# Expert stage: weights in 8 KB rows, six half-unit slots, the whole down projection in split fp32r, the next expert's tokens transposed and split one expert ahead

## The reference

```python
def expert_choice_ffn(h, w_router, w_gate, w_up, w_down):
    B, N, D = h.shape                                    # 1, 1024, 1024
    cap = EC_CAPACITY_FACTOR * N // N_EXPERTS            # 128
    aff = softmax(einsum('bnd,de->bne', h, w_router), axis=-1)
    gates, idx = lax.top_k(aff.swapaxes(1, 2), cap)
    xe = h[bidx, idx]
    hid = silu(einsum('becd,edf->becf', xe, w_gate)) * einsum('becd,edf->becf', xe, w_up)
    ye = einsum('becf,efd->becd', hid, w_down) * gates[..., None]
    return zeros_like(h).at[bidx, idx].add(ye)
...
        x = x + g2 * expert_choice_ffn(...)
    return rms_norm(x, final_norm_g)
```

## Time and profile before

| | us |
|---|---|
| median of three runs | 2294.64 |
| the runs | 2291.88 to 2295.27 |
| span of the profiled execution, first to last instruction | 2290.7 |
| from one expert to the next, experts 1 to 14 | 73.2 |
| PE, VectorE, ScalarE busy, whole span | 2040.5, 1425.3, 1139.4 |

### The profile page before, as it was taken

One profiled execution on the slowest core, in us unless ns is written; L12 is line 12 of the kernel. 1 busy time (PEld: TensorE's weight loads), 2 busy tenths in 40 slices (PEclk: granted clock), 3 DMA queues, 4 the chain that ended last, 5 costly groups with the idle time before them and its releaser, 6 DMA issues.

```text
span 2290.7 us, 26943 instructions
## 1 busy us (share of the span) xinstructions
PE 2040.5 (89%) x8729; PEld 1439.4 (63%) x8729; DVE 1425.3 (62%) x1852; ACT 1139.4 (50%) x1764; POOL 233.8 (10%) x305
## 2 busy tenths in 40 slices
PE   5899988899899988951999999999999999999993
PEld 2444475566666666631777777777777777777772
DVE  0355430577767677637677767777676767777673
ACT  1222110566756576621565555566565555656552
POOL 0222100011111011111000000000000000000001
PEclk9999999899999999975999999999999999999997
DMA  8311183401111011023999999999999999999994
GB/s 273 123 74 73 55 280 119 123 26 47 56 55 39 25 46 55 27 70 132 344 344 350 354 374 361 349 347 383 357 352 350 354 373 362 348 348 371 358 360 162
DMA packets 220443, 515.32 MB, mean 225 GB/s; under 512 B 9416, under 2 KB 34416, under 8 KB 219248
## 3 DMA queue, kind: packets, MB, share of 16 engines
q1 hardware_dynamic: 212880, 491.44, 58.5%
q0 software_dynamic: 4608, 16.78, 2.8%
q10 hardware_dynamic: 2912, 6.55, 0.7%
HBM read 481.19 MB, written 33.55 MB: 225 GB/s over the span
## 4 chain that ended last, share of the span: by engine, by line
PE 46%; DVE 3%; issue 3%; DMA 1%; ACT 1%; POOL 0%; SPq 0%; ACTq 0%; POOLq 0%
PE banks L1390 30%; PE banks L1420 8%; PE banks L1416 2%; PE banks L1418 2%; PE banks L1417 2%; DVE w_lo L1290 2%; ACT w_hi L1185 1%; PE banks L1400 1%; PE banks L1371 1%; DMA munit<-acc_scratch 1%; DVE topi L1259 1%; DVE top L1257 0%; DVE cand L1260 0%; DMA xe<-h_scratch,idx_g 0%; DMA acc_scratch<-ysc,idx_s 0%
## 5 line engine op out<-in xcount | busy, mean ns | idle before, releaser
L1290 DVE TENSOR_TENSOR w_lo<-munit,w_hi 128x2048 fp32r<-128x2048 f32 x256 | 573.8, 2288 | 130.5 <-ACT w_hi L1185 130.5
L1185 ACT ACTIVATE w_hi<-munit 128x2048 fp32r<-128x2048 f32 x256 | 473.5, 1915 | 141.0 <-DMA munit<-in_w_up 103.5
L1390 PE MATMUL banks<-w_hi,x_hi 128*128 128x512 f32 x1024 | 427.5, 418 | 27.3 <-DVE w_lo L1290 25.9
L1390 PE MATMUL banks<-w_hi,x_lo 128*128 128x512 f32 x1024 | 401.0, 392 | 0.0
L1390 PE MATMUL banks<-w_lo,x_hi 128*128 128x512 f32 x1024 | 399.5, 390 | 0.0
L1390 PEld LDWEIGHTS banks<-w_hi,x_hi 128*128 128x128 f32 x1024 | 192.9, 188 | 87.1 <-DVE w_lo L1290 37.1
L1420 PE MATMUL banks<-munit,hidt 128*128 128x512 f32 x512 | 240.6, 592 | 0.0
L1390 PEld LDWEIGHTS banks<-w_lo,x_hi 128*128 128x128 f32 x1024 | 193.3, 189 | 48.0 <-issue 11.2
L1390 PEld LDWEIGHTS banks<-w_hi,x_lo 128*128 128x128 f32 x1024 | 192.7, 188 | 42.6
L890 DVE TENSOR_TENSOR ptl<-banks,pth 128x384 fp32r<-128x384 f32 x320 | 176.4, 554 | 53.6 <-ACT pth L836 49.2
L836 ACT ACTIVATE pth<-banks 128x384 fp32r<-128x384 f32 x320 | 157.1, 491 | 75.0 <-PE banks L986 66.9
(11 more groups left out here) (191 smaller groups left out, 2631.7 us busy)
## 6 DMA issues: line engine op xcount, KB each, us to landing
munit<-in_w_gate SPq DMA_DIRECT2D x64, 2048.0 KB, 8.7
munit<-in_w_up SPq DMA_DIRECT2D x64, 2048.0 KB, 13.5
munit<-in_w_down SPq DMA_DIRECT2D x64, 2048.0 KB, 14.5
unit<-in_w_mod SPq DMA_DIRECT2D x12, 1024.0 KB, 7.5
q_scratch<-qst SPq DMA_DIRECT2D x8, 1536.0 KB, 5.6
win<-in_w_mod SPq DMA_DIRECT2D x12, 1024.0 KB, 12.4
qt<-q_scratch SPq DMA_DIRECT2D x32, 384.0 KB, 4.1
dft<-in_dft SPq DMA_DIRECT2D x4, 1026.0 KB, 10.8
```

Of the source, the lines that this page charges most:

```text
L1185: act.activation(w_hi[which][c][:, :], unit[k0 % NU][:, c * CH:(c + 1) * CH], ACT.Copy).then_inc(s["hi_done"], 1)
L1290: dve.tensor_tensor(w_lo[which][c][:, :], unit[(3 * j + which) % NU][:, c * CH:(c + 1) * CH], w_hi[which][c][:, :].bitcast(F32), ALU.subtr ...
L1390: i = pe.matmul(psum[:, 2 * (j % 2) + which, :], x_[:, k, :], w_, start=(k == 0 and w_ is hi and x_ is x_hi), stop=(k == KD - 1 and x_ is ...
```

## The change

- On the host the three weight tensors are packed into one, `w_exp`, in which each half unit of 1 MB is 128 rows of 8 KB, one for each partition.
- The four slots of 2 MB become six slots of 1 MB, `raw[w][c]`, for gate, up and down with two halves each. A slot has one kind of load, and it is loaded again as soon as its own `lo_done` or `d_lo_done` has come.
- `down` takes all four k-tiles in split form: 24 fp32r matmuls, four `d_hi`, four `d_lo`, and `h_hi` and `h_lo` for 512 columns. `hidt` and the fp32 product fall away. `down_mm`, `gate_mm` and `up_mm` are counted by k-tile or half.
- `split_down` of the step before moves ahead of silu on ACT, and ahead of `turn` on both ACT and DVE. `sil`, `hid`, `h_hi` and `h_lo` have one buffer in place of two.
- `x_hi` and `x_lo` have two sets. The transposes of expert e + 1 and their `x_part` are done in steps 1 and 2 of expert e, one half in each, between `turn` and `project(e, j, 1)`.
- `result(e - 1)` stands at the start of step 1 on DVE, which is next to the place that it had at the end of step 0.
- The loops over the experts run in pairs. GpSimd's code is not changed.

```diff
+def expert_weights(w_gate, w_up, w_down):
+
+    j = DE // UC
+    g, u = (w.reshape(E, 2, KD // 2, P, j, UC).transpose(0, 4, 1, 3, 2, 5).reshape(E, j, 2, P, KD * UC // 2) for w in (w_gate, w_up))
+    d = w_down.reshape(E, j, 2, UC // P // 2, P, D).transpose(0, 1, 2, 4, 3, 5).reshape(E, j, 2, P, UC // P // 2 * D)
+    return np.stack([g, u, d], axis=2)
...
-    unit = [sb(f"munit{i}", [P, KD * UC], F32, M) for i in range(NU)]
+    raw = [[sb(f"raw{w}{c}", [P, CH], F32, M) for c in range(2)] for w in range(3)]
...
-    x_hi, x_lo = (sb(f"x_{n}", [P, KD, P], F32R, M) for n in ("hi", "lo"))
+    x_hi, x_lo = ([sb(f"x_{n}{i}", [P, KD, P], F32R, M) for i in range(2)] for n in ("hi", "lo"))
...
         def _(sp):
+            def load(e, j, w, c):
+                st = NJ * e + j
+                if w < 2:
+                    after(sp, s["lo_done"], 4 * (st - 1) + 2 * w + c + 1 if not isinstance(st, int) or st > 0 else 0)
+                else:
+                    after(sp, s["d_lo_done"], NK * (st - 1) + 2 * c + 2 if not isinstance(st, int) or st > 0 else 0)
+                sp.dma_start(raw[w][c][:, :], w_exp[e][j, w, c]).then_inc(raw_in[w][c], 16)
+
+            def expert(e, par, first, last):
                 for j in range(NJ):
...
+                    for w in range(2):
+                        load(e, j, w, 0)
+                        load(e, j, w, 1)
+                    if not (first and j == 0):
+                        load(*step_before(e, j), 2, 0)
+                        load(*step_before(e, j), 2, 1)
...
         def _(act):
-            def expert(e, first, last):
+            def expert(e, par, first, last):
                 for j in range(NJ):
+                    if not (first and j == 0):
+                        split_down(*step_before(e, j))
                     gate(e, j)
...
+                    if not (first and j == 0):
+                        turn(*step_before(e, j))
+                    if not last and j in (1, 2):
+                        x_part(e + 1, 1 - par, j - 1)
+                    if not (last and j == NJ - 1):
+                        for which in range(2):
+                            split(*step_after(e, j), which, 0)
+                            split(*step_after(e, j), which, 1)
...
         def _(dve):
-            def expert(e, first, last):
+            def expert(e, par, first, last):
                 for j in range(NJ):
...
+                    if j == 1 and not first:
+                        result(e - 1)
+                    if not (first and j == 0):
+                        split_down(*step_before(e, j))
+                        turn(*step_before(e, j))
+                    if not last and j in (1, 2):
+                        x_part(e + 1, 1 - par, j - 1)
+                    if not (last and j == NJ - 1):
+                        split(*step_after(e, j), 0, 0)
+                        split(*step_after(e, j), 0, 1)
                     hidden(e, j)
...
         def _(pe):
+            def down(e, j):
...
+                for k in range(NK):
+                    pe.wait_ge(s["d_lo_done"], NK * st + k + 1)
+                    for x_, w_ in ((h_hi, d_hi), (h_hi, d_lo), (h_lo, d_hi)):
+                        for h in range(2):
+                            i = pe.matmul(psum[:, Y + h, :], x_[:, k, :], w_[k][:, h * 512:(h + 1) * 512],
...
                     i.then_inc(s["down_mm"], 1)
...
+            def expert(e, par, first, last):
                 for j in range(NJ):
...
+                    project(e, par, j, 0)
+                    if not (first and j == 0):
+                        turn(*step_before(e, j))
+                    if not last and j in (1, 2):
+                        x_turn(e + 1, j - 1)
+                    project(e, par, j, 1)
+                    if not (first and j == 0):
+                        down(*step_before(e, j))
```

More of the change, by code:

```diff
@@ L1054, in nc_phase_m @@
     xe = sb("xe", [P, D], F32, M)
-    x_hi, x_lo = (sb(f"x_{n}", [P, KD, P], F32R, M) for n in ("hi", "lo"))
+    x_hi, x_lo = ([sb(f"x_{n}{i}", [P, KD, P], F32R, M) for i in range(2)] for n in ("hi", "lo"))
     w_hi, w_lo = ([[sb(f"w_{n}{i}{c}", [P, CH], F32R, M) for c in range(2)] for i in range(2)] for n in ("hi", "lo"))
[L1058 to L1063, removed]
+    sil = sb("sil", [P, UC], F32, M)
+    hid = sb("hid", [P, UC], F32, M)
+    h_hi, h_lo = (sb(f"h_{n}", [P, NK, P], F32R, M) for n in ("hi", "lo"))
+    d_hi, d_lo = ([sb(f"d_{n}{k}", [P, D], F32R, M) for k in range(NK)] for n in ("hi", "lo"))
     ysc = sb("ysc", [P, D], F32, M)
@@ L1344, in _ @@
                 if which == 0:
[L1345 to L1351 removed]
+                    x_part(0, 0, 0)
+                    x_part(0, 0, 1)
+            every(expert, dve)
+            split_down(E - 1, NJ - 1)
+            turn(E - 1, NJ - 1)
             result(E - 1)
@@ L1396, in turn @@
                 pe.wait_ge(s["hid_done"], st + 1)
-                after(pe, s["ht_done"], st)
                 after(pe, s["h_lo_done"], st)
-                for k in range(4):
-                    i = pe.transpose(psum[:, HB, k * P:(k + 1) * P], hid[j % 2][:, k * P:(k + 1) * P], ident[:, :])
+                if isinstance(e, int) and e == 0 and j == 0:
+                    pe.wait_ge(s["x_b"], 2)
+                for k in range(NK):
+                    i = pe.transpose(psum[:, HB, k * P:(k + 1) * P], hid[:, k * P:(k + 1) * P], ident[:, :])
@@ new lines, in down @@
+                pe.wait_ge(s["h_lo_done"], st + 1)
+                if j == 0:
+                    after(pe, s["y_done"], e)
+                for k in range(NK):
+                    pe.wait_ge(s["d_lo_done"], NK * st + k + 1)
+                    for x_, w_ in ((h_hi, d_hi), (h_hi, d_lo), (h_lo, d_hi)):
+                        for h in range(2):
+                            i = pe.matmul(psum[:, Y + h, :], x_[:, k, :], w_[k][:, h * 512:(h + 1) * 512],
+                                          start=(j == 0 and k == 0 and x_ is h_hi and w_ is d_hi),
+                                          stop=(j == NJ - 1 and k == NK - 1 and x_ is h_lo))
```

254 lines of the change are left out of this document (83 added, 171 removed).

## The result

The changed kernel takes 2417.36 us in the median of four runs (2415.47 to 2420.15), the kernel before on the same chip 2294.95 us (2291.88 to 2297.1). The ratio is 1.0537, with a 95% interval of 1.0524 to 1.0550: slower, by 122 us. The predicted 2349 us had the sign, and the time lies above the range. The profiled execution of the changed kernel has a span of 2413.4 us.

What follows compares the result with a forecast made beforehand. PE was taken as the bound, DMA close behind. Experts 1 to 14 go from 73.2 to 68.3 + 7.7 + 2.0 = 78.0 us, +67; offset -12.5; total +55 on 2290.7: 2345, as median 2349, range 2308 to 2392.

Steps and rivals of the forecast that it cites:

- rival 2: No stall at all in step 1, the advance split is hidden: -81 us, 2213 us; chance 5%.
- 8 KB rows, value zero: Weight loads in 8 KB rows: about 413 GB/s, 61 us an expert, hidden under PE, so no gain and no loss.
- `y_done`: VectorE makes it in step 1, from T1 its start: `ysc` ends at T1+2.45, PE comes to its transposes at T1+5.93.
- The tail: End of expert 15: PE's wait for d_lo falls from 4.2 to some 2.5 us without clock drop, 3.3 us better.
- C: Cost of PE's half-speed clock behind the stall, per expert: 1.65 to 2.35 us, taken as 2.0.
- S: PE's stall for the gather before step 1's transposes, experts 1 to 14: 0.2 + L, 5.4 to 9.4 us, taken as 7.7.
- L: Time from the gather's issue to its landing: 5.2 us to loaded rows of 8.6 median, taken as 7.5.
- 3.44 from `carry` to the issue of the gather: GpSimd's time behind `ysc` in step 1, from `carry` to issuing the gather: 3.44 us, read from the profile before.
- 1: Gather early enough and clock holds: S + C = 5.4, 2289 us; the change gains below 5.8; chance 5%.
- rival 3: Long weight rows hold up scatter and gather on the DMA engines: +3.6 us on L, 2399 us; chance 11%.
- 4: VectorE becomes the bound, half a microsecond over PE's step in three steps of 15 experts: 2371 us; chance 4%.
- 5: 8 KB rows move slower and bind below 345 GB/s; at 320 GB/s 87 us more, 2436; chance 2%.

Runs made afterwards that it cites:

- late_turns: Changed kernel with the next expert's token transposes and their x_part in steps 2 and 3 instead of 1 and 2: 2208.49 us, ratio 0.9621 to the kernel before.
- gather_ahead: Changed kernel with GpSimd gathering two experts ahead, before the scatter; transposes stay in steps 1 and 2: 2208.5 us, ratio 0.9618 to the kernel before.
- late_rows_2k: late_turns with the weights unpacked as in DRAM, 2 KB rows for gate and up, 4 KB for down: 2206.38 us.
- rows_2k: Changed kernel with the weights unpacked as in DRAM, 2 KB rows for gate and up, 4 KB for down, same six slots: 2406.79 us.
- hold_down_loads: Changed kernel with the two down loads of step 1 issued only after the gather has landed, in experts 1 to 14: 2351.16 us.
- turn_first: Changed kernel with VectorE doing h_lo ahead of the four d_lo in step 1: 2339.64 us.
- turn_hold: Changed kernel with both edits, h_lo before d_lo in step 1 and that step's down loads held until the gather has landed: 2336.18 us.
- hold_up_and_down_2: turn_first with step 2's up loads issued only after the w_lo of its gate, step 1's down loads queued behind them: 2309.75 us.
- turn_hold_fill: turn_hold with 24 extra fp32r matmuls, result unread, before PE's wait for the gather in experts 1 to 14: 2311.51 us.
- late_old_down: late_turns with the old down projection, two k-tiles in split fp32r and two in plain fp32 from the slot: 2253.85 us.

## Why the prediction was right or wrong

Right, and shown:

- *Which part decides.* The moved transposes bring a wait for the gather in step 1 of experts 1 to 14, behind `ysc`, scatter and gather. late_turns and gather_ahead each take it away, and with it 209 us.
- *The rest of the change.* Without a stall the prediction has 2213 us (rival 2's figure); measured, 2208.5. A period of 68.02 us answers to 68.3, and the fp32r down to 45 of 47 us.
- *8 KB rows, value zero*, as long as nobody waits for the gather. late_rows_2k is 2 us from late_turns, inside their runs' spread. At full load late_turns moves 418 to 434 GB/s, more than the 413 of the earlier trace rows, and PE covers it. In the kernel after their value isn't zero: rows_2k is 11 us faster.
- *`y_done`.* PE came to its transposes 3.52 us after `ysc` ended (1501.20 - 1497.68); 3.48 had been worked out.
- *The tail.* PE waits 2.57 us there, for 2.5 predicted, and 4.18 before.
- *The clock, C = 2.0.* It is 1.9 in the mean of the 14 places. The single places spread over 1.4 to 2.9, wider than the bounds of 1.65 and 2.35.

Wrong were the two terms of S behind `ysc`, and above all the landing of the gather. At the place shown, S is 0.23 + 7.23 + 8.50 + 0.25 - 3.52 = 12.69 us; the prediction had 0.2 + 3.44 + 7.5 - 3.48 = 7.7.

- *"I take 7.5"* for L, the landing, is the step that failed. It rests on the argument that nobody runs ahead and the loads run dry behind the last two down halves. They do run dry, but only behind the landing (0 GB/s from 1513.9); while scatter and gather were under way 382 and then 245 GB/s were still moving. The rows at full load had said 8.6; here the median is 8.8 and the mean 9.1, and behind the short hold-up 10.3. The down loads in flight are the cause: with these two held back (hold_down_loads) the landing is 5.3 and the stall 7.65, 4.9 less, though GpSimd's hold-up is still there, and the time is 2351 us. That this is the predicted 7.7 and 2349 is luck: the distance to the issue is 5.24 for 3.44 and the landing 5.3 for 7.5.
- *"3.44 from `carry` to the issue of the gather"* was read where VectorE was idle behind `ysc`. The change puts four `d_lo` there, and the distance is 6.5 us in the mean, 3.0 more. turn_first restores 3.42. What this costs is far less than 3.0: within the kernel after, 2.0 us less of it come back as 1.8 us more of landing, and with the down loads held turn_hold gains 0.5 us by it. The Trainium skill, "SBUF — State Buffer", section "Who interferes with whom", says that a VectorE instruction with two inputs in SBUF contends with a GpSimd one that reads SBUF. `d_lo` and `carry` are such a pair, and the trace agrees: 4.36 against 0.19 us. The page speaks of a lock held for one whole instruction, and says so of VectorE's two-port modes; here `carry` lasted to the end of a row of four at nine of 14 places. That the cause is this port, and not something else that ends with the row, no run here isolates.

The two terms aren't independent, which the sum had taken for granted: the same loads that a later issue waits out are those that an earlier one meets. In turn_hold 1.8 us earlier became 0.55 us less of stall.

In all: (12.6 - 7.7) x 14 = 69 us too little by S, (1.9 - 2.0) x 14 = -1 by C, less 5 for the base of 2213: 63 of the 68 us between 2417 and 2349. The sum for the kernel after falls short by as much, and where that comes from is open.

The rivals: 1 never came: its point of S + C = 5.8 was reached by no kernel that keeps the wait. The least is (2310 - 2208)/14 = 7.3, in hold_up_and_down_2 and near it in turn_hold_fill, both 0.7 to 0.8% slower than before. 2 didn't happen. 3 gave a time near the measured one (2399), but its mechanism is only a small part of it: with short rows the stall is still 11.8 us, 4.1 over the predicted one. It isn't nothing either: the packed rows cost the landing 0.6 us in the kernel after and 2.1 to 2.3 in late_turns, for the 3.6 that rival 3 had. The Trainium skill, "DMA: Bandwidth & Descriptors", section "Queues, rings and completion order", says that a DMA engine drains a whole packet of one ring before it switches to the next. If longer rows make longer packets, a gather waits longer behind 8 KB rows; the landings at equal hold-up agree in direction (10.3 against 9.75 us, 11.7 against 9.4), and no run shows the turns themselves. 4 and 5 are refuted by late_turns: there PE is busy 400 of 400 us and the loads keep up.

Left open: how much of a landing each load in flight costs (it took 11.8 us in late_old_down, where it is issued 4.63 us behind `carry` beside a full load), why the packed rows cost the gather 0.6 us in one pair of kernels and over 2 in the other, and what the hold-up of GpSimd is at bottom.

## What to carry to other kernels

When a consumer moves earlier, follow its producer back to where that is released, in whichever queue it stands, before the change is made: here the gather stood behind a scatter, which stood behind work at the start of the very step in which its data were now wanted. Read each duration on that path under the load that it will have, not at the place where it stands today; a quiet neighbour and an idle queue are part of the number. Read it at every place, too: the clock's cost at one wait was 2.9 us, and 1.9 in the mean of 14. And give a prefetch its own slot in the order: the same change with the transposes one step later, or with the gather one expert ahead, is 3.8% faster than the kernel before, where it was 5.4% slower.

## What the runs showed of the hardware

- A one-column GpSimd operation beside VectorE's two-input fp32 subtractions of 128x1024 took about 0.95 us (5 of 14 places) or 4.36 to 4.46 (9), ending with the first or the fourth of them, and 0.19 us without them (turn_first).
- The same 0.5 MB gather takes 5.0, 5.3, 6.7, 6.9 or 8.8 us from issue to landing, with more and more weight loads in flight beside it. In the kernel after one issued 2.0 us earlier takes 1.8 us longer (10.3 and 8.5).
- Beside a full load the gather takes 11.7 us with weights in 8 KB rows and 9.4 with 2 and 4 KB rows, issued at the same distance behind `carry` (late_turns, late_rows_2k).
- A wait of 5.4, 7.2 or 12.6 us of PE costs 1.8, 2.3 or 1.9 us behind it by the lower clock, in the mean of 14.
- 50 matmuls into an unused bank kept the granted clock at 1.00 through 13 of 14 waits of over 10 us, and brought 25 us (1%) in all.
- At full load one core moved 418 to 434 GB/s in 8 KB rows (late_turns, 1520 to 1544 us), against 386 in 2 KB rows; the windows of 400 us moved 384 and 385 GB/s with either, since PE set the pace.
